# Branch products of two mixers in three float32r passes: four more weight splits in each, two engines on the heads' outputs

## The reference

```python
def mixer_block(x, w_in, b_gate, rpb, sink, w_branch_na, w_branch_sw, w_out):
    ...
    y_na = neighbourhood_attention(hs(q_na, NA_HEADS), hs(k_na, NA_HEADS), hs(v_na, NA_HEADS), rpb)
    ...
    y_sw = sliding_window_attention(qs, ks, hs(v_sw, SW_KV_HEADS), sink)
    y_na = y_na @ w_branch_na
    y_sw = y_sw @ w_branch_sw
    gates = jax.nn.sigmoid((gate_logits + b_gate).astype(jnp.float32)).astype(x.dtype)
    g_na, g_sw = jnp.split(gates, N_BRANCHES, axis=-1)
    return (g_na * y_na + g_sw * y_sw) @ w_out
```

## Time and profile before

| | us |
|---|---|
| median of 3 runs | 2176.8 (2176.19 to 2179.8) |
| the profiled execution | 2179.22 |
| its span, first to last instruction | 2177.4 |
| PE busy in the span | 2115.4 (97%) |
| PE weight loads | 1848.3 (85%) |
| DVE busy | 1555.5 (71%) |
| ACT busy | 1173.3 (54%) |
| mean granted TensorE clock | 0.990 |

### The profile page before, as it was taken

How to read it: one execution, slowest core, us unless ns; L and a number is a source line. 1 busy time by engine, 2 the same in 40 slices (tenths; PEclk the granted TensorE clock), 3 DMA queues, 4 the chain that set the end, 5 groups by cost and what they waited for, 6 DMA issues and landing times.

```text
span 2177.4 us, 33158 instructions
## 1 busy us (share of the span) xinstructions
PE 2115.4 (97%) x12570; PEld 1848.3 (85%) x12570; DVE 1555.5 (71%) x1823; ACT 1173.3 (54%) x1201; POOL 9.8 (0%) x22
## 2 busy tenths in 40 slices
PE   7999998999999989999999999999999999999997
PEld 6888897999898889989888888888888888888885
DVE  8677354655645464464548989899898989899897
ACT  3301134443446343343635777777777777777774
POOL 0000000000000000000000000000000000000000
PEclk9999999999999999999999999999999999999998
DMA  8344342455462345555335989899898989899893
GB/s 312 127 155 135 115 155 96 175 184 185 186 227 109 136 169 180 193 205 201 117 130 200 375 340 371 348 362 366 340 368 345 365 338 364 348 365 370 348 360 154
DMA packets 76181, 540.01 MB, mean 248 GB/s; under 512 B 9136, under 2 KB 9280, under 8 KB 11952
## 3 DMA queue, kind: packets, MB, share of 16 engines
q1 hardware_dynamic: 71856, 522.22, 62.6%
q0 software_dynamic: 2080, 10.40, 1.3%
q10 hardware_dynamic: 2144, 5.93, 0.7%
HBM read 537.47 MB, written 1.05 MB: 247 GB/s over the span
## 4 chain that ended last, share of the span: by engine, by line
PE 87%; DVE 8%; ACT 2%; issue 2%; DVEq 1%; DMA 0%; ACTq 0%
PE psum L1319 14%; PE psum L929 11%; PE psum L1296 9%; PE psum L1300 9%; PE psum L1299 9%; PE psum L767 6%; PE psum L942 5%; PE psum L741 5%; PE psum L707 4%; PE psum L694 2%; DVE scan_t L2194 2%; DVE scan_t L2197 1%; DVE big L2200 1%; PE psum L720 1%; PE psum L754 1%
## 5 line engine op out<-in xcount | busy, mean ns | idle before, releaser
L2405 DVE TENSOR_TENSOR w_l<-ring,w_h 128x2048 fp32r<-128x2048 f32 x336 | 769.1, 2291 | 104.0 <-ACT w_h L1505 97.9
L1505 ACT ACTIVATE w_h<-ring 128x2048 fp32r<-128x2048 f32 x336 | 645.5, 1921 | 131.7 <-PE psum L1296 92.4
L1296 PE MATMUL psum<-w_h,xe_h 128*128 128x512 f32 x896 | 359.3, 401 | 0.9 <-DVE w_l L2405 0.9
L1300 PE MATMUL psum<-w_h,xe_l 128*128 128x512 f32 x896 | 349.8, 390 | 0.0
L1299 PE MATMUL psum<-w_l,xe_h 128*128 128x512 f32 x896 | 349.5, 390 | 0.0
L2025 DVE TENSOR_TENSOR wf_l<-ring,wf_h 128x2048 fp32r<-128x2048 f32 x66 | 151.2, 2292 | 135.9 <-ACT wf_h L1496 135.9
L1996 DVE TENSOR_TENSOR wp_l<-ring,wp_h 128x2048 fp32r<-128x2048 f32 x52 | 119.0, 2291 | 128.3 <-ACT wp_h L1519 128.3
L1296 PEld LDWEIGHTS psum<-w_h,xe_h 128*128 128x128 f32 x896 | 168.3, 188 | 37.0 <-DVE w_l L2405 4.1
L1300 PEld LDWEIGHTS psum<-w_h,xe_l 128*128 128x128 f32 x896 | 168.2, 188 | 36.1
L929 PE MATMUL psum<-xf_h,wf_h 128*128 128x256 f32 x688 | 195.7, 285 | 1.7 <-DVE xf_l L2033 1.7
L1299 PEld LDWEIGHTS psum<-w_l,xe_h 128*128 128x128 f32 x896 | 168.6, 188 | 31.8
(11 more groups left out here) (424 smaller groups left out, 3682.4 us busy)
## 6 DMA issues: line engine op xcount, KB each, us to landing
ring<-in_stream SPq DMA_DIRECT2D x497, 1024.0 KB, 6.1
big<-in_bc POOLq DMA_DIRECT2D x11, 512.0 KB, 8.1
big<-in_na_bias POOLq DMA_DIRECT2D x2, 2048.0 KB, 9.3
h<-in_x SPq DMA_DIRECT2D x2, 512.0 KB, 4.3
big<-in_mem ACTq DMA_DIRECT2D x1, 1024.0 KB, 12.5
big<-in_s_c ACTq DMA_DIRECT2D x1, 1024.0 KB, 13.3
r_k<-in_sgu_ln ACTq DMA_DIRECT2D x1, 1024.0 KB, 17.9
out_dram<-ysum ACTq DMA_DIRECT2D x2, 512.0 KB, 2.6
```

Of the source, the lines that this page charges most:

```text
L1296: first = nc.tensor.matmul(out, xe_h[:, k, :], wh[:, i, :], start=(k == 0), stop=False)
L1300: last = nc.tensor.matmul(out, xe_l[:, k, :], wh[:, i, :], start=False, stop=(k == KD - 1))
L1505: nc.scalar.activation(high, src, ACT.Copy).then_inc(w_high, 1)
L2405: V.tensor_tensor(low, src, high.bitcast(F32), ALU.subtract).then_inc(w_split, 1)
```

## The change

The branch products go over to the split form. `split_plan` lists the four branch chunks of each mixer between w_in and w_out, so each mixer has four more `wp_part` on ACT and four more `wp_rest` on DVE. `split_a4` takes the place of `form_a4` there: 48 float32r matmuls in a chunk for 32 instructions. The activations need a high and a low part too. For the neighbourhood half DVE makes both out of onT (on_h, a cast into the space of hf_l, and on_l, a difference), behind negm and `wp_rest` of pair 5. For the window half ACT's copy out of PSUM gives the high part (os_h), and DVE makes the low part from the same bank (`low_of_pair`), which it then frees in ACT's place: of pairs 4 and 5 ahead of the sums of pairs 6 and 7, of pairs 6 and 7 behind the attention and ahead of `wp_rest`. 12 KB per partition that were reserved go to the three new parts. DVE's two casts for the router (L2350, L2351) move behind the branches.

```diff
@@ split_plan @@
+        out += [(("k4", f"w_{n}_{m}", c), (f"b{n}{m}", 2 * c + 1)) for n in ("na", "sw") for c in range(2)]
@@ PE @@
+            def split_a4(name, chunk, x_h, x_l, u0):
+                n = SPLIT_AT[chunk]
+                pe.wait_ge(wp_split, n + 1)
+                wh, wl = (w.rearrange("p (k c) -> p k c", k=4) for w in wp_slot(n))
+                for u in range(2):
+                    open_unit(pe, (name, u0 + u))
+                    for j in range(2):
+                        cols = slice((2 * u + j) * P, (2 * u + j + 1) * P)
+                        for k in range(4):
+                            for i, (w, x) in enumerate(((wh, x_h), (wh, x_l), (wl, x_h))):
...
                 def first_branch():
-                    evacuated(pe, (f"at{m}_o", 3))
-                    form_a4(f"bna{m}", ("k4", f"w_na_{m}", 0), onT, 0)
+                    pe.wait_ge(on_split, m + 1)
+                    split_a4(f"bna{m}", ("k4", f"w_na_{m}", 0), on_h, on_l, 0)
...
-                form_a4(f"bna{m}", ("k4", f"w_na_{m}", 1), onT, 2)
+                split_a4(f"bna{m}", ("k4", f"w_na_{m}", 1), on_h, on_l, 2)
                 evacuated(pe, (f"at{m}_o", PAIR_N - 1))
                 for c in range(2):
-                    form_a4(f"bsw{m}", ("k4", f"w_sw_{m}", c), osT, 2 * c)
+                    split_a4(f"bsw{m}", ("k4", f"w_sw_{m}", c), os_h, os_l, 2 * c)
@@ ACT @@
-                        free_unit(nc.scalar.activation(dst_of(j - 1), bank(u)[:, 0:TOK], ACT.Copy, scale=0.5), u)
+                        last = nc.scalar.activation(dst_of(j - 1), bank(u)[:, 0:TOK], ACT.Copy, scale=0.5)
+                        if j - 1 < 4:
+                            free_unit(last, u)
+                        else:
+                            last.then_inc(os_high, 1)
...
-                merged_high(4 + 4 * m)
+                for _ in range(3):
+                    wp_part()
+                merged_high(4 + 4 * m, (0, 1))
+                wp_part()
+                merged_high(4 + 4 * m, (2, 3))
                 for _ in range(2):
                     wp_part()
@@ DVE @@
                     if i in (3, 5, 7):
                         wp_rest()
+                    if i == 5:
+                        evacuated(dve, (name + "_o", 3))
+                        V.tensor_copy(on_h, onT).then_inc(on_high, 1)
+                        dve.wait_ge(on_high, m + 1)
+                        V.tensor_tensor(on_l, onT, on_h.bitcast(F32), ALU.subtract).then_inc(on_split, 1)
+                    if i >= 6:
+                        low_of_pair(name, m, i - 2)
                     dve.wait_ge(exp_ready, g0 + i + 1)
...
+                for j in (PAIR_N - 2, PAIR_N - 1):
+                    low_of_pair(name, m, j)
+
+            def low_of_pair(name, m, j):
+                u = (name + "_o", j)
+                take_unit(dve, u)
+                dve.wait_ge(os_high, 4 * m + j - 3)
+                last = V.scalar_tensor_tensor(os_l[:, j - 4, :], bank(u)[:, 0:TOK], 0.5, os_h[:, j - 4, :].bitcast(F32),
+                                              ALU.mult, ALU.subtract)
+                free_unit(last, u)
...
                 wp_rest()
-                if m == 1:
-                    V.tensor_copy(before_r[:, :], before)
-                    link(V.tensor_copy(ones_r[:, :], ones[:, :]))
                 evacuated(dve, (f"gb{m}", PAIR_N - 1))
                 for i in range(4):
                     take_unit(dve, (f"bna{m}", i))
...
+                    if i % 2 == 1:
+                        wp_rest()
                 for i in range(4):
                     take_unit(dve, (f"bsw{m}", i))
...
                     merged_rest(f"out{m}", i)
+                    if i % 2 == 1:
+                        wp_rest()
+                if m == 1:
+                    V.tensor_copy(before_r[:, :], before)
+                    link(V.tensor_copy(ones_r[:, :], ones[:, :]))
```

More of the change, by code:

```diff
@@ L332, in build @@
             hf_l = operand("hf_l", [P, 2, 2, TOK])
-            dense.enter_context(nc.sbuf_tensor("constants_stay_1", [P, 8192], F32))
+            o_parts = operand("o_parts", [P, 3, 4, TOK])
+            dense.enter_context(nc.sbuf_tensor("constants_stay_1", [P, 5120], F32))
             xf_h = operand("xf_h", [P, KD, TOK])
@@ L422, in build @@
         v_sw = view(r_k, 1280, 256, "p (b d) -> p b d", b=TB)
-        osT = view(r_zu, 0, 1024, "p (k t) -> p k t", t=TOK)
+        on_h = hf_l[:, :, :, :].rearrange("p a b t -> p (a b) t")
+        on_l, os_h, os_l = (o_parts[:, n, :, :] for n in range(3))
         slot_full = [sem(f"slot_full{i}") for i in range(SLOTS)]
@@ L471, in build @@
         bgate_halved = sem("bgate_halved")
+        on_high = sem("on_high")
+        on_split = sem("on_split")
+        os_high = sem("os_high")
         rexp_in = sem("rexp_in")
@@ L712, in form_a4 @@
                                 release(last, chunk)
+                    close_unit(last, (name, u0 + u))
+            def split_a4(name, chunk, x_h, x_l, u0):
[8 more added lines that the diff above has]
+                            for i, (w, x) in enumerate(((wh, x_h), (wh, x_l), (wl, x_h))):
+                                last = nc.tensor.matmul(bank((name, u0 + u))[:, j * TOK:(j + 1) * TOK], w[:, k, cols],
+                                                        x[:, k, :], start=(k == i == 0), stop=(k == 3 and i == 2))
+                                if u == j == k == i == 0:
+                                    release(last, chunk)
                     close_unit(last, (name, u0 + u))
@@ L1519, in wp_part, with merged_high @@
                 nc.scalar.activation(wp_slot(n)[0], ring[:, at % SLOTS, :], ACT.Copy).then_inc(wp_high, 1)
-            def merged_high(m0):
-                for i in range(4):
+            def merged_high(m0, parts=range(4)):
+                for i in parts:
                     act.wait_ge(m_ready, m0 + i + 1)
@@ L1742, in gate_b @@
                                                    bias=bgate[:, m, 8 + j:9 + j], scale=0.5), u)
-                pair_attention(f"at{m}", lambda j: (onT if j < 4 else osT)[:, j % 4, :],
+                pair_attention(f"at{m}", lambda j: (onT if j < 4 else os_h)[:, j % 4, :],
                                lambda i: sink_col(m, i - 8) if i >= 8 else None, gate_b)
-                merged_high(4 + 4 * m)
+                for _ in range(3):
[3 more added lines that the diff above has]
+                merged_high(4 + 4 * m, (2, 3))
                 for _ in range(2):
@@ L1955, in attention, with pair_attention @@
                         xf_rest_of((name + "_o", i - 2), "x_o", i - 2, xq_h, xq_l)
-            def pair_attention(name, bias_of, sink_of):
+            def pair_attention(name, m, bias_of, sink_of):
                 g0 = head0[name]
@@ L2345, in _ @@
                 dve.wait_ge(loads["nab"], 16 * (m + 1))
-                pair_attention(f"at{m}", lambda i: nabias[:, i, :, :] if i < 8 else swmask,
+                pair_attention(f"at{m}", m, lambda i: nabias[:, i, :, :] if i < 8 else swmask,
                                lambda i: sink_col(m, i - 8) if i >= 8 else None)
                 wp_rest()
-                if m == 1:
-                    V.tensor_copy(before_r[:, :], before)
-                    link(V.tensor_copy(ones_r[:, :], ones[:, :]))
                 evacuated(dve, (f"gb{m}", PAIR_N - 1))
```

## The result

| us | before | changed |
|---|---|---|
| median (6 runs each, side by side) | 2177.11 (2174.89 to 2179.8) | 2191.51 (2190.14 to 2194.1) |
| the profiled execution | 2179.22 | 2194.1 |
| its span | 2177.4 | 2192.3 |
| PE busy | 2115.4 (97%) | 2113.2 (96%) |
| DVE busy | 1555.5 (71%) | 1578.8 (72%) |

What follows compares the result with a forecast made beforehand. PE, busy 97%, was taken to bound the kernel. Net of its saving, 4.7 us later per mixer gave 9.4; with 3.0 for the clock, 12.4 on a median of 2176.8 made 2189.2, range 2183 to 2196.

Steps and rivals of the forecast that it cites:

- PE's own saving: Branch chunks on PE: 5.75 us in place of 6.97, 1.22 less each, 9.8 less over four chunks in two mixers.
- DVE in the attention: First mixer's attention: DVE's added work starts pair 6 2.5 us late, pair 7 3.5 late; the attention ends 2.0 later.
- PE's wait ahead of the output of pair 5: In the attention: PE waits 1.6 us for ACT's copy of the transposes of pair 5.
- The wait ahead of the second w_na chunk: Behind the attention: PE waits 3.1 us, as DVE makes the low part of pair 7 before this chunk's split.
- The wait ahead of the first w_out chunk: Behind the branches: PE waits 2.6 us for DVE's split of this chunk, until 752.4.
- From out0 to out1: Start of first to start of second w_out chunk: DVE sets the pace, from 752.4 to 760.1.
- T7 to the second w_out chunk: From the transposes of pair 7 to that chunk on PE: 38.4 us without the clock, 35.6 before.
- The clock: Behind the 3.1 us wait PE falls to 1.2 GHz: 1.5 us per mixer, 3.0 in all; nothing behind the 2.6.
- (1): Rival: waits in attention and behind it cost less and the clock stays up, 7.4 us slower, 2184; chance 0.17.
- (2): Rival: clock falls also behind the 1.6 wait and around the 2.6, up to 6 us more, 2195; chance 0.15.
- (4): Rival: saving and waits cancel over the kernel, about no difference; chance 0.04.
- (3): Rival: no waits behind the attention, matmul saving arrives less the attention's delay, -5.8 us, 2171; chance 0.04.

Runs made afterwards that it cites:

- F: Changed kernel with A, B and E together, and splits, gatings and sums behind the attention in order of readiness; 2170.71 beside 2179.39 before, ratio 0.9963.
- B: Changed kernel with DVE's onT parts moved behind negm of pair 6 and low parts behind the multiplications; 2187.88 beside 2178.01 before, ratio 1.0046.
- G: F with the attention's DVE work left as in the changed kernel; 2173.68 beside 2177.66 before, ratio 0.998.
- A: Changed kernel with DVE's split of the second w_na chunk ahead of the low part of pair 7; 2182.4 beside 2178.01 before, ratio 1.0022.
- E: Changed kernel with the first w_sw and first w_out chunks split into idle dense-layer buffers; 2187.02 beside 2179.39 before, ratio 1.0037.
- C: Changed kernel with six unused plain products on PE ahead of its wait for the second w_na chunk; 2191.01 beside 2178.01 before, ratio 1.0061.
- D: Changed kernel with all its waits and splits, but plain branch products from the ring; 2204.48 beside 2178.01 before, ratio 1.0128.

## Why the prediction was right, point by point

The forecast was 2189.2, in a range of 2186 to 2192 for its own sum; 2191.51 was measured. Its steps one by one:

- **PE's own saving** (5.75 in place of 6.97 a chunk): right. 5.75 stands in the chains above, and F brings 9.2 of the 9.8 us. The Trainium skill's 109 ns for 256 columns (TensorE: Matmul & The Clock Gate, Back-to-back issue gap) would, as an estimate, have made it 5.24. The page gives that for an isolated matmul and says that in a stream of weight loads and matmuls both set the spacing; the trace has such a stream, at 5.75 / 48 = 0.120 us.
- **DVE in the attention**: right to a tenth. Less the 0.26 us by which this execution is late, pair 6 starts at 707.65 (forecast 707.6), pair 7 at 714.67 (714.6), T7 at 721.83 (721.7). The cast took 0.69, not 0.63. PE's wait ahead of the output of pair 5 is 1.68 (1.6). B shows that it is the place of these operations that costs. G, in which nothing behind the attention waits, still has their 2.1 us per mixer (2.0), so they lie on the path.
- **The wait ahead of the second w_na chunk**: 3.21, forecast 3.1, released by DVE's wp_l. A shows it by taking it away.
- **The wait ahead of the first w_out chunk**: 2.53, forecast 2.6; the row names no releaser, but in the chain DVE's wp_l ends at 755.71, 0.1 ahead of it. E shows that the buffer's turn was the reason. From out0 to out1 it is 7.68 (7.7) in both mixers, with the clock at 0.54 behind the wait in the one and at 1.00 in the other, so that the lower clock there costs nothing, as the forecast had it.
- **T7 to the second w_out chunk**: 38.4 without the clock was forecast; C, which keeps the clock up, has 38.78. With the attention's 2.1 the two mixers of C are 10.7 longer than before where 9.4 was forecast, 1.3 more. It is small change, per mixer: 0.3 from the transposes of pair 7 to the second w_na chunk (11.07 for 10.8), 0.2 in the three chunks (17.5 for 17.3), 0.1 less in the wait behind them, 0.1 in the attention, and 0.1 to 0.2 in rounding and in the 35.6 of before, which is 35.52 on PE's timeline.
- **The clock**: the mechanism was right, its size was not. I took 1.5 in each mixer, from the one stretch behind the idle time of 3.50. C measures 2.6 in the first mixer and 1.5 in the second, 4.1 for 3.0. This is the term of the sum that was mis-sized: 1.1 of the 2.5 us by which the traces exceed it (14.9 for 12.4); 1.3 are the steps above. By the medians the excess is 2.0. Two readings behind the term were too simple. The stretch does not always begin where PE starts again: behind the same idle time of 3.50 the kernel before has its second mixer's eight transposes at full clock (1.09) and the lower one only 1.3 us later. And the idle time of 1.79 was not free of it: in E the transposes behind it took 1.80. The rows, of the kernel before and of E:

```profile
1061.71 1.09 PE L898 MATMUL psum<-ident,r_zv 128*128 128x128 f32 x8 [3.50 <-DVE r_zv L1985]
```

```profile
779.55 1.80 PE L706 MATMUL psum<-ident,h 128*128 128x128 f32 x8 [1.79 <-DVE h L1950]
```

  That one sample of 1.5 came so near the 1.5 and 2.6 of the two places is in part luck.
- **The rivals.** The waits did not cost less (1). The clock did not fall behind the wait of 1.68 (1.00 in the window above), and where it fell behind that of 2.53 it cost nothing, so (2) did not happen either, though the longer stretch in the first mixer goes its way. (4), that saving and waits cancel, did not happen: the saving was there (D), and the waits had the size worked out. (3), the saving that arrives, was named with its condition: no wait ahead of the second chunk, and w_out's first chunk split early. G meets that condition with the attention's delay left in, and has -5.5 in its span and -4.0 by the timed runs where -5.8 was worked out. The Trainium skill advises to optimize the engine of highest occupancy first (Perfetto Trace Analysis, Identifying the Most-Contended Engine); it judges TensorE's headroom by the share of peak FLOPs and by the weight loads' busy share, and the latter is 85% here beside DVE's 71%, so that the engine is the same. Followed alone it was not enough: the work taken off PE counted once the other two engines' orders had been laid around it, and turned into 14 us of loss before that.

## What to carry to other kernels

When a product that reads its weights straight from a ring gets an operand that two other engines must make first, cost the order of those engines before the product: ask of each new operation what it waits for, and what PE will need next that is queued behind it. Here the matmuls were 9.8 us cheaper, and two statements in the wrong order on DVE, one double buffer, one early cast and the order of splits and gatings behind the attention cost 24. If such a change loses, look for the wait in the chain and move the statement before giving up the change; A and B were each worth, to a few tenths of a microsecond in the traces, what their waits and the clock behind them measured, and E its wait and 0.7 us more per mixer.

## What the runs showed of the hardware that I had not expected

The same wait of 3.21 us was followed by the lower clock for longer in the first mixer (0.50, then 0.64 in the two windows of 3.4 us) than in the second (0.52, then 1.00), with the same instructions around it; the price was 2.6 against 1.5 us. It came again in a second execution of the same kernel, and in E as 2.6 and 1.6, but other edits changed it: 1.5 in both mixers in B, 1.5 and then 2.7 in D. The 36.5 us behind the first mixer's second w_out chunk show the same thing (mean clock 0.91 or 0.86 with the same idle times of PE, 1.2 us apart). And the length of the idle time does not decide by itself: behind 2.53 us the clock was 0.54 in one mixer and 1.00 in the other, and behind 1.79 eight transposes took 1.09 in the kernel before, in the changed one and in all the others but E, where they took 1.80. Whether a short idle time costs anything beyond itself can thus depend on what an edit does elsewhere. So the total of an edit worth 2 us does not tell its worth, while the distance between two of PE's instructions came again to 0.1 us. Why a stretch is long at one place and short at the other stays open.
